# A streaming encoder layer on one core: the first token group holds the 64 sample tokens alone

## What is computed

```python
z  = rmsnorm(x) @ w_in          # q, k, v | f, i, q, g of HGRN2 | gate_a, gate_b
x  = x + ((sigmoid(gate_a) * (o_a @ w_a) + sigmoid(gate_b) * (o_b @ w_b)) @ w_out)
# peer(x): s = scores of 8 heads against two sets of 128 sub-keys, top 16 of each, top 16 of the 256 sums
hid = gelu(einsum('nd,nhkd->nhk', xb, u_tab[ib]))
out = einsum('nhk,nhkd->nd', gate * hid, v_tab[ib])
y  = rmsnorm(x + out, norm_final)
```

## Time and profile before

| | |
|---|---|
| time, median of 3 runs | 4907.48 us (4901.1 to 4922.41) |
| span of the profiled execution | 4927.5 us |
| busy: DVE, POOL, PE, ACT | 3792.1, 3035.1, 2016.8, 643.0 us |
| DMA moved | 1401.80 MB, 284 GB/s |
| head | 583 us |
| stretches 1 to 4 | 995, 995, 1012, 914 us |
| tail | 428.5 us |

### The profile page before, as it was taken

The page is one execution under the profiler, slowest core; times in us unless marked ns, Lnnn a source line. Parts: engine busy times, 40 slices in busy tenths (PEclk is TensorE's granted clock), DMA queues, the critical chain, the costliest instruction groups (busy, mean ns, idle before and its releaser), DMA issues. The chain is left out here.

```text
span 4927.5 us, 36538 instructions
## 1 busy us (share of the span) xinstructions
PE 2016.8 (41%) x8760; PEld 1702.8 (35%) x8760; DVE 3792.1 (77%) x7049; ACT 643.0 (13%) x1480; POOL 3035.1 (62%) x2637
## 2 busy tenths in 40 slices
PE   3867265546121776462205873631134523210000
PEld 3756254435120565351205662531124422210000
DVE  0234987686999786978996869789978697888777
ACT  1211121111001221110011211110011110000000
POOL 0000177466876676667766666677677677787777
PEclk7768567768565668586656585865565756655555
DMA  5314389779887999899879997998799999988998
GB/s 131 128 62 143 90 197 225 198 216 366 296 308 247 346 376 335 282 358 330 290 262 326 350 357 268 341 350 286 260 336 366 381 323 361 343 299 309 325 317 295
DMA packets 529920, 1401.80 MB, mean 284 GB/s; under 512 B 47760, under 2 KB 223376, under 8 KB 528976
## 3 DMA queue, kind: packets, MB, share of 16 engines
q0 software_dynamic: 317856, 1149.91, 67.4%
q1 hardware_dynamic: 210656, 245.41, 15.7%
q10 hardware_dynamic: 1232, 4.46, 0.2%
HBM read 1379.68 MB, written 19.92 MB: 284 GB/s over the span
## 5 line engine op out<-in xcount | busy, mean ns | idle before, releaser
L531 POOL DMA_INDIRECT ring<-in_peer_u,ixs x1152 | 1426.5, 1238 | 913.5 <-DVE hid L1464 490.3
L531 POOL DMA_INDIRECT ring<-in_peer_v,ixs x1152 | 1420.1, 1233 | 525.0 <-issue 345.2
L1470 DVE SCALAR_TENSOR_TENSOR acc<-ring,wk,acc 128x1024 f32<-128x1024 f32 (+1 forms) x1152 | 1476.0, 1281 | 203.2 <-DMA ring<-in_peer_v,ixs 190.5
L1464 DVE CUSTOM_DVE_ANT_0 ring<-ring,xt 128x1024 f32<-128x1024 f32 (+1 forms) x1152 | 1402.3, 1222 | 268.3 <-DMA ring<-in_peer_u,ixs 195.5
L587 PE MATMUL PS<-xnT,wring 128*128 128x256 f32 (+2 forms) x3840 | 862.8, 393 | 992.5 <-ACT tmp L1065 852.9
L587 PEld LDWEIGHTS PS<-xnT,wring 128*128 128x128 f32 x3840 | 757.7, 223 | 1093.6 <-issue 950.3
L546 POOL DMA_DIRECT2D xt<-xn_scr x9 | 5.5, 610 | 424.0 <-DMA xn_scr<-tmp 423.9
L591 PE MATMUL PS<-wring,xnT 128*128 128x256 f32 (+1 forms) x864 | 227.9, 430 | 79.3 <-DMA wring<-in_w_in 79.3
L591 PEld LDWEIGHTS PS<-wring,xnT 128*128 128x128 f32 (+1 forms) x864 | 181.1, 213 | 125.3 <-DMA wring<-in_w_in 86.1
L591 PE MATMUL PS<-wring,M 128*128 128x256 f32 (+1 forms) x576 | 152.4, 431 | 112.7 <-DVE tmp L1371 77.1
L587 PE MATMUL PS<-Q,wring 128*128 128x256 f32 (+2 forms) x640 | 141.1, 378 | 105.5 <-DVE M L1185 43.6
(11 more groups left out here) (175 smaller groups left out, 2587.0 us busy)
## 6 DMA issues: line engine op xcount, KB each, us to landing
wring<-in_w_in SPq DMA_DIRECT2D x110, 1024.0 KB
wring<-in_peer_query SPq DMA_DIRECT2D x40, 1024.0 KB
wring<-in_w_out SPq DMA_DIRECT2D x20, 1024.0 KB
ring<-in_peer_u,ixs POOLq DMA_INDIRECT x1152
ring<-in_peer_v,ixs POOLq DMA_INDIRECT x1152
bias<-rel_scr SPq DMA_DIRECT2D x80, 144.0 KB
wring<-in_w_branch_a SPq DMA_DIRECT2D x10, 1024.0 KB
wring<-in_w_branch_b SPq DMA_DIRECT2D x10, 1024.0 KB
```

The costliest lines, as they stand in the source:

```text
L531: pool.indirect_dma_start(ring[0:rows, n % R, :], None, (u_tab, v_tab)[kind], bass.IndirectOffsetOnAxis(ap=ixs[0:rows, kind, k:k + 1], axi ...
L1464: dve.tensor_tensor_reduce(row, row, xt[0:rows, s, :], 1.0, 0.0, ALU.mult, ALU.add, hid[0:rows, q % 2, k:k + 1]).then_inc(ring_used, 1)
L1470: dve.scalar_tensor_tensor(out=acc[0:rows, s, :], in0=row, scalar=wk[0:rows, q % 2, k:k + 1], in1=acc[0:rows, s, :], op0=ALU.mult, op1=ALU ...
```

## The change

Only `GROUPS` is written in another way. The sample tile stands alone in group 0 with 64 columns; the eight prompt tiles follow in four groups of two, all of 256 columns. The number of groups and of weight passes stays five.

```diff
-GROUPS = [[(SAMPLE, 64, 0), (0, 128, 64)], [(1, 128, 0), (2, 128, 128)], [(3, 128, 0), (4, 128, 128)],
-          [(5, 128, 0), (6, 128, 128)], [(7, 128, 0)]]
+GROUPS = [[(SAMPLE, 64, 0)], [(0, 128, 0), (1, 128, 128)], [(2, 128, 0), (3, 128, 128)],
+          [(4, 128, 0), (5, 128, 128)], [(6, 128, 0), (7, 128, 128)]]
```

## The result

The changed kernel takes 5028.1 us (median of 4 runs, 4981.5 to 5033.0) against 4914.8 us for the kernel before (4 runs, 4901.1 to 4922.4): 1.0205 times as long, with a 95% interval of 1.015 to 1.026. It is slower, as the forecast's sign said, but by 113 us instead of the 27 us of the sum, and the time lies above the stated range (4902 to 4990 us). The profiled execution of the changed kernel has a span of 5030.1 us (its own time 5031.9), where the sum of the prediction made 4954.5 us out of before's span of 4927.5.

A forecast was written before the change was run, and what follows sets the result against it. DVE was taken as nearest to the bound beside expert rows, POOL as full in the tail. Terms -226 - 264 + 98 + 419 = +27 us on 4927.5 gave 4954.5, at the median 4935; range 4902 to 4990 us.

The forecast's parts named there:

- the head: Opening span where the first group's stages run without expert rows: 357 us instead of 583, 226 less.
- I take 3.65: In the head, a 1 MB weight block of 32 64-column instructions takes 3.65 us, between bounds 1.9 and 3.81.
- The other doubt: In the head, weight blocks might need 4.2 us each; over 28 such blocks that gives +15 us.
- Rival 2: In the head, TensorE's clock stays low; ten tokens-stationary blocks take 7.1 instead of 3.6 us: +35, total 4970; chance 0.10.
- Stretch 1: Second group's two full tiles' stages beside 256 expert rows instead of 512: 731 us instead of 995, 264 less.
- Rival 1: Stretch 1 stays as thick with waiting as before: 768 us, 37 more, total 4972; chance 0.15.
- Stretches 2 to 4: Three stretches with two full tiles' stages beside 512 expert rows: 3019 us instead of 2921, 98 more.
- the tail: Closing expert rows with no other work, 512 instead of 256, at 1.64 us each: 419 us more.
- Rival 3: DVE's waits in stretch 1 swallow the expert rows whole: stretch under 679 us, total down to 4774; chance 0.09.
- The step to the median: Whole kernel: profiled run lies 20 us above the timed median, so +27 is added to 4907.5, giving 4934.5.

The follow-up runs named there:

- pad128: Changed kernel with the first group's weight-stationary matmuls streaming 128 columns instead of 64, the additional columns holding unread ones: 4953.1 us, 1.0044 times before.
- pad192: Changed kernel with the first group's weight-stationary matmuls streaming 192 columns instead of 64, the additional columns holding unread ones: 4996.4 us, 1.0130 times before.
- sample_last_pad: sample_last with the sample group's weight-stationary matmuls 128 columns wide, nothing else different: 5000.0 us, 1.014 times before.
- single_second: Kernel before with groups reordered: first group as before, one tile alone second, then three pairs of tiles: 5077.4 us, 1.0301 times before.
- sample_last: Kernel before with groups replaced: four pairs of prompt tiles first, sample tile alone last, its recurrence starting from the prompt's state: 4999.1 us, 1.0194 times before.
- hot64: Changed kernel with 16 extra 256-column instructions, results overwritten, ahead of each weight-stationary product's 64-column ones in the first group: 5119.5 us in one run.

## Why the prediction was wrong

**The step that failed** is the price of a weight block in the head, "I take 3.65". The row behind it, 3.81 us for 128 columns, was taken for the upper end, since half the columns could not cost more. But that row was measured at the upper level, and the thin blocks ran at the lower: 7.04 us measured. The kernel before around that row, 4198.25 us:

```profile
4198.00:4202.00 4.00, 3.75 (x33) 3.78 (x34) 4.00 (x15) 0.28 (x2) 0.93 (x1) 1.00 1.07 366
```

The other doubt, that a block might need 4.2 us for its weights, looked at the wrong cause and gave +15 as the upper end, where the stages show +76:

| stage | predicted | measured | pad128 |
|---|---|---|---|
| end of B | 103 | 114 | 105 |
| C | 46 | 43 | 43 |
| D | 22 | 43 | 26 |
| E | 29 | 44 | 29 |
| F | 32 | 33 | 33 |
| G | 22 | 42 | 26 |
| H | 23 | 22 | 22 |
| I | 80 | 92 | 84 |
| end of the head | 357 | 433 | 368 |

28 blocks at 7.04 - 3.65 = 3.4 us are 95 us of PE time. In B, D, E and G, where PE is the pace, 20 blocks make 68 us and the four stages are 67 us over; in I most of it hides beside the top-k: the stage is 12 us over, 8 of which padding takes off. With 128 columns, pad128, every stage is within 4 us of the prediction.

**Rival 2** named the right mechanism and priced it wrong. It gave the lower level to the ten blocks with the tokens stationary (+35) and said "the weight blocks would still hide it". Both halves were the wrong way round: the blocks with the tokens stationary are where the clock rises, and four of them took 15.87 us in E, 4.0 each instead of 7.1; the weight blocks are what the lower level doubles. Nor does PE idle from block to block, as the rival has it; the clock is low while PE is busy. Changed kernel, E's four blocks (timeline), then short pieces of E, H and I:

```profile
227.27 15.87 PE L591 MATMUL PS<-wring,xnT 128*64 128x256 f32 x64
...
224.00:227.00 3.00, 3.00 (x16) 3.00 (x15) 0.00 (x0) 0.18 (x1) 0.00 (x0) 0.50 0.30 106
227.00:231.00 4.00, 4.00 (x11) 2.29 (x11) 0.00 (x0) 0.22 (x1) 0.00 (x0) 0.50 0.62 198
231.00:235.00 4.00, 4.00 (x20) 2.48 (x19) 0.00 (x0) 0.38 (x1) 0.00 (x0) 1.00 0.44 119
...
331.00:335.00 4.00, 4.00 (x20) 2.38 (x18) 0.42 (x1) 0.00 (x0) 0.00 (x0) 1.00 1.02 318
...
345.00:350.00 5.00, 5.00 (x25) 5.00 (x25) 0.00 (x0) 0.45 (x2) 1.27 (x2) 0.50 0.39 112
```

Until 227 us PE runs thin weight blocks at 0.50, then the wide instructions of E's other blocks, and some us into them the row shows 1.00; the same in H (331 to 335); with the thin blocks of I it is 0.50 again. The rival's chance of 0.10 was too small: PE's first instructions after its long wait stood in the earlier trace rows, ten of them in 3.54 us, 354 ns each. The same width took about 35.31/206 = 171 ns in D, at 0.92, and takes 5.36/32 = 168 ns at 0.91 in pad192. So the rows at hand showed that a weight instruction has two prices. The Trainium skill (TensorE: Matmul & The Clock Gate, "HAM oscillation — how this bites in real kernels") lets the clock drop in the waits for weights. This trace doesn't show that: in D it is 0.50 with 0.56 us of idle time ahead of the first block and no wait for weights. It was low before D, in C (0.55), and before G, in F (0.56), where PE waits again and again for ACT or DVE and is busy for 30.83 of 43 and 17.05 of 33 us; the thin blocks of D and G then ran at 0.50 to their end. Padding is one of two remedies that the section gives for a thin M, there to 512 or more. In pad128 the thin operand was padded to 128 columns, and that took 76 us off the median (5028.9 to 4953.1); 65 us of it are the head (433 to 368), the rest lies in parts that vary from run to run.

**What was right.** Stretch 1 took 734 us for 731; C took 104 for 97, F 117 for 112, I 225 for 231, the others within 3:

```profile
513.00:617.00 104.00, 37.82 (x121) 26.12 (x122) 88.01 (x147) 21.41 (x70) 75.88 (x70) 0.52 0.87 204
728.00:845.00 117.00, 50.08 (x211) 38.26 (x212) 100.35 (x147) 21.85 (x48) 39.91 (x42) 0.55 0.34 94
942.00:1167.00 225.00, 77.84 (x320) 66.09 (x320) 205.89 (x658) 26.16 (x76) 86.98 (x74) 0.68 0.48 136
```

Rival 1 (768) didn't come. Stretches 2 to 4 took 3017 for 3019, the tail 846 for 848. Rival 3 would have needed stretch 1 under 679. That the terms hold to 3 us is in part luck: misses of 7, 5 and -6 us nearly cancel in stretch 1, and the tail of 512 rows took anything from 809 to 846 us in the runs above.

**The step to the median.** The sum was made on spans, and 20 us were taken off because before's profiled run lay that far above its median. The changed kernel's profiled run lies 2 us from its median, so of the 93 us between 4935 and 5028.1 some 76 are the head and most of the rest is this correction. Before's median itself was 4928.4, 4906.9 and 4914.4 in later comparisons; a span of one run is not a better basis than that.

## What to carry to other kernels

When a change makes the operand of a weight-stationary matmul thinner, price its blocks at both clock levels, with the row that shows the lower one as the upper end; a PE that will be busy is no reason to count on the upper level. If the stage is bare of other work, try the thin operand padded: here 128 columns cost hardly more than 64 at the upper level, and the head got 65 us shorter; beside rows that set the pace (sample_last_pad) it won nothing. And what a tile's stages or rows cost depends on their company. Adding up stage by stage from rows with the same company held within 3 us for three terms here and within 13 us in single_second but for its tail, and it missed stretch 4 of sample_last by 73 us or more. Why the change loses at all is in the table of stretches: the 150 us of the head and 261 of stretch 1 that it saves are less than the 96 of stretches 2 to 4 and the 417.5 of a tail with nothing beside it that it adds.

## What the runs showed of the hardware

- PE stayed at a granted clock of 0.50 through stages D and G with 64-column fp32 instructions, busy in 41.89 of 43 and 41.23 of 42 us, and was at 0.88 and 0.87 with 128-column ones at the same places.
- An fp32 instruction with a new weight block took 108 ns with 64 columns (hot64) and about as long with 128 (3.74 us for 32 in pad128) at the upper level, and 213 to 217 ns with 64 at the lower. At 192 columns it is 5.36 us for 32.
- The same 512 expert rows alone took between 809 and 846 us from run to run.
